# The end of the experts and the query norms of a two-block network: an earlier branch, column groups, weights split in the wait

## The reference

```python
def hier_moe(h, ...):                       # h: 768 rows in layer 0, 512 in layer 1
    # each row goes to 2 of 32 experts, with weights w
    y = sum_over_2( w * (silu(x @ w_gate[e]) * (x @ w_up[e])) @ w_down[e] )
x = x + g2 * y                              # in both layers
h = rmsnorm(x, norm_mix_g[1]) * (1 + sc1) + sh1          # start of layer 1
q, k, v, cq, ckv, kr = split(h @ w_in)
q = rope(rmsnorm(q.reshape(..., 4, 128), q_g))           # a norm per head
k = rope(rmsnorm(k.reshape(..., 2, 128), k_g))
# after layer 1: x = rmsnorm(x, final_norm_g), then rmsnorm(x, norm_ffn1) @ ffn1_w1, ffn1_w3
```

## Time and profile before

| | us |
|---|---|
| three runs | 3094.8, 3103.38, 3102.12 (median 3102.12) |
| the profiled execution | 3101.73 |
| its span in the trace | 3099.9 |
| PE busy | 2854.0 (92%) |
| VectorE, ScalarE, GpSimd busy | 1075.6, 754.5, 503.1 |
| mean granted TensorE clock | 0.949 of 2.4 GHz |

### The profile page before, as it was taken

How to read it: one execution, slowest core, us unless ns; L and a number is a source line. 1 busy time by engine, 2 the same in 40 slices (tenths; PEclk the granted TensorE clock), 3 DMA queues, 4 the chain that set the end, 5 groups by cost and what they waited for, 6 DMA issues and landing times.

```text
span 3099.9 us, 37034 instructions
## 1 busy us (share of the span) xinstructions
PE 2854.0 (92%) x15818; PEld 2010.1 (65%) x15818; DVE 1075.6 (35%) x2095; ACT 754.5 (24%) x1299; POOL 503.1 (16%) x503
## 2 busy tenths in 40 slices
PE   6989899989969899979999996999999889999997
PEld 4777756445457666765645445888875556788876
DVE  4973310000034644331010004333355654432334
ACT  4142211101123144221110113222211164331223
POOL 0000133322210034113332221000033051000000
PEclk9999999999969999979999997999999999999998
DMA  7613999999942132279999983323311201332321
GB/s 275 202 45 119 361 383 407 411 408 411 392 164 68 57 109 109 82 297 365 413 414 417 416 362 126 109 96 95 123 58 38 94 15 55 95 109 82 109 87 43
DMA packets 140522, 621.53 MB, mean 200 GB/s; under 512 B 14127, under 2 KB 95151, under 8 KB 106688
## 3 DMA queue, kind: packets, MB, share of 16 engines
...
## 4 chain that ended last, share of the span: by engine, by line
PE 74%; DMA 12%; DVE 7%; ACT 2%; issue 2%; POOL 1%; PEld 1%; DVEq 0%; SPq 0%; POOLq 0%; PEldq 0%; ACTq 0%
PE ps L92 71%; DMA ring<-in_exp_up,wix 8%; DMA hT<-in_exp_up,wix 3%; PE ps L95 3%; DVE scr L114 2%; ACT hT L98 1%; DVE scr L106 1%; DMA ring<-in_mod_w 1%; DVE scr L120 1%; PEld ps L92 1%; DVE ring_r L106 1%; DVE scr L117 0%; DVE hT_r L106 0%; DVE hT L114 0%; POOL yrows L139 0%
## 5 line engine op out<-in xcount | busy, mean ns | idle before, releaser
L92 PE MATMUL ps<-ring_r 128*128 128x512 f32 (+1 forms) x2688 | 779.4, 376 | 22.2 <-DVE hT_r L106 21.5
L92 PEld LDWEIGHTS ps<-ring_r 128*128 128x128 f32 x2688 | 496.9, 191 | 129.5 <-issue 35.7
L92 PE MATMUL ps<-ring,scr 128*64 128x512 f32 (+4 forms) x1984 | 447.8, 547 | 40.0 <-DMA ring<-in_mod_w 23.7
L92 PE MATMUL ps<-hT_r,ring_r 128*128 128x512 f32 (+1 forms) x1256 | 472.8, 376 | 0.0
L92 PEld LDWEIGHTS ps<-ring,scr 128*64 128x64 f32 (+2 forms) x1984 | 163.4, 145 | 236.8 <-issue 223.9
L106 DVE TENSOR_TENSOR scr<-scr,ps 64x512 f32<-64x512 f32 (+1 forms) x76 | 52.4, 690 | 761.7 <-ACT scr L98 434.2
L92 PE MATMUL ps<-scr_r,ring_r 128*128 128x512 f32 x1312 | 306.7, 390 | 0.3 <-issue 0.3
L92 PEld LDWEIGHTS ps<-scr_r,ring_r 128*128 128x128 f32 x1312 | 246.3, 188 | 52.3 <-issue 0.5
L92 PEld LDWEIGHTS ps<-hT_r,ring_r 128*128 128x128 f32 x1256 | 240.9, 192 | 43.3 <-issue 2.0
L106 DVE TENSOR_TENSOR ring_r<-ring,ring_r 128x2048 fp32r<-128x2048 f32 (+1 forms) x98 | 216.1, 2228 | 73.4 <-ACT ring_r L102 73.0
L102 ACT ACTIVATE ring_r<-ring 128x2048 fp32r<-128x2048 f32 (+1 forms) x102 | 186.4, 1835 | 181.2 <-DMA ring<-in_ffn_w 132.0
...
## 6 DMA issues: line engine op xcount, KB each, us to landing
...
```

Of the source, the lines that this page charges most:

```text
L92: return self.real.matmul(o, l, r, start=start, stop=stop) if self.real else Quiet()
```

## The change

- `overflow` takes `instead`, which is run in the branch without further blocks. GpSimd now drains and branches before the scatter of block 31; the scatter is the first thing in either branch. "further" is counted in the branch.
- SyncE issues the two early weights ahead of its wait for the results, and each tile's results in one transfer of 1 MB instead of two of 512 KB.
- ScalarE makes the early upper parts, then loads the table of the square root, before it weighs tile 0. VectorE makes the lower parts before its first sum of rows; GpSimd makes none. The gains of the next norm (`dve_gains`) and of the two norms (`dve_two_gains`) are computed there too.
- `sums`: the squares are the moving operand (128 columns), the stationary one has 32 columns (ones, or the gains in columns 0 and 1 of 32 and zeros), and the eight matmuls go to four groups of 32 rows of PSUM, two into each. ScalarE copies the 128x128 out (`groups`), and one matmul by `group_sum` adds the four groups into a column (`total_columns`), in PE's order one tile later.
- `act_adaln`: the upper part of the first input tile comes ahead of the shift of the second.
- Heads: the squares are the stationary operand, a column of ones goes through (`norm_sum`), so a sum is a column of 128 tokens. Root and reciprocal are taken on 128x4 or 128x2, and PE spreads the result with four or two matmuls (`norm_root`) at the position after; VectorE copies it to SBUF and scales. The rotation comes one position later.

```diff
-POOL_LOWER = [("at", 0), ("at", 1), ("ffn1_", 1, 0), ("ffn1_", 3, 0)]
...
-    def overflow(self, flag, body, *own):
+    def overflow(self, flag, body, *own, instead=None):
...
         with self.real.Else():
+            if instead:
+                self.met = dict(met)
+                instead()
...
-    def dve_adaln(e, name, l, which, gname, T, st, two=None, normed=False):
+    def dve_gains(e, name, l, which, gname):
...
+    def dve_adaln(e, name, l, which, gname, T, st, two=None, normed=False, gains=True):
+        if gains:
+            dve_gains(e, name, l, which, gname)
...
             act_norm(e, st)
-        for kt in range(9 if two else 8):
-            if kt < 8:
-                for r, (a, n) in enumerate(chunks(T)):
-                    e.wait_ge(*root_took(st, a, kt == 7, h_scaled, name, kt, a))
-                    i = e.activation(H(kt, a, n), H(kt, a, n), ACT.Identity, bias=mod(l, which, kt, r))
-                i.then_inc(*h_ready.up(name, kt))
-            if two and kt >= 1:
-                e.wait_ge(*h_ready.of(name, kt - 1))
-                e.copy(two(kt - 1)[0], H(kt - 1, 0, T)).then_inc(*h_hi.up(name, kt - 1))
+        def upper(kt):
+            e.wait_ge(*h_ready.of(name, kt))
+            e.copy(two(kt)[0], H(kt, 0, T)).then_inc(*h_hi.up(name, kt))
+        for kt in range(8):
+            for r, (a, n) in enumerate(chunks(T)):
+                e.wait_ge(*root_took(st, a, kt == 7, h_scaled, name, kt, a))
+                i = e.activation(H(kt, a, n), H(kt, a, n), ACT.Identity, bias=mod(l, which, kt, r))
+            i.then_inc(*h_ready.up(name, kt))
+            if two and kt != 1:
+                upper(max(kt - 1, 0))
+        if two:
+            upper(7)
...
         e.memset(Two.eps2, EPS ** 2)
+        e.tt(Two.gn, vec("fin_g", 0, 8), vec("n1", 0, 8), MUL)
+        e.tt(Two.g2, vec("fin_g", 0, 8), vec("fin_g", 0, 8), MUL)
+        step(e, e.memset(Two.gains, 0.0))
         e.memset(Two.gains[:, :, 0:1], 1.0)
-        step(e, e.tt(Two.g2, vec("fin_g", 0, 8), vec("fin_g", 0, 8), MUL))
-        e.ts(Two.gains[:, :, 1], Two.g2, EPS, ADD)
-        e.tt(Two.gn, vec("fin_g", 0, 8), vec("n1", 0, 8), MUL).then_inc(*dve_step.up("two_gains"))
+        e.ts(Two.gains[:, :, 1], Two.g2, EPS, ADD).then_inc(*dve_step.up("two_gains"))
...
                 wr.take(expert_slot(kind, b), "e", l, kind, b)
+        for key in early[l]:
+            early_load(e, key)
...
         for i in range(M.NT):
-            for q in range(2):
-                r = 768 * q + 128 * i
-                e.dma(moe_y(l, i, q), yrows[r:r + 128, :]).then_inc(*y_in[i].up(l, q, by=16))
+            e.dma(moe_y(l, i).rearrange("p (q c) -> p q c", q=2), yrows.rearrange("(q t p) c -> t p q c", q=2, p=128)[i]).then_inc(
+                *y_in[i].up(l, by=16))
+    def early_load(e, key):
+        if key[0] == "at":
+            raw_load(e, 3 + key[1] % 3, key, *At.jobs[key[1]])
+        else:
+            ffn_load(e, ffn1, ffn1.jobs.index(key[1:]))
...
                 store(b - 1)
-        store(31)
...
         first, end = 32, M.NB
+        pool_outputs(e, l, 31, *y_out[1].up(l, 31, by=16))
...
         e.wait_ge(*ov_y[l][(end - 1) % 2].of(l, end - 1))
+        e.drain().then_inc(*pool_step.up("further", l))
...
-    def moe_y(l, i, q):
...
+    def moe_y(l, i):
+        a = 2048 * i
         if l == 0:
-            return ring[:, 1024 * n:1024 * n + 1024]
-        return (hT[:, 1024 * n:1024 * n + 1024] if n < 6 else moes[l].xr[n - 6])
+            return ring[:, a:a + 2048]
+        return hT[:, a:a + 2048] if i < 3 else moes[l].xr01
...
                     c = 512 * h + 128 * j
-                    m = e.transpose(o[:, 128 * j:128 * j + 128], moe_y(l, i, 0)[:, c:c + 128], k("id"))
+                    m = e.transpose(o[:, 128 * j:128 * j + 128], moe_y(l, i)[:, c:c + 128], k("id"))
...
         def sums(i):
+            o = ps.take("y_square", l, i)
+            e.wait_ge(*ps.ready("y_square", l, i))
             e.wait_ge(*squared.of(st_m[l].name, i))
+            if l:
+                e.wait_ge(*dve_step.of("two_gains"))
+            for c in range(8):
+                j = c % 4
+                m = e.matmul(o[32 * j:32 * j + 32, 0:128], Two.gains[:, c, :] if l else k("ones")[:, 0:32],
+                             M.xt[i % 2][:, 128 * c:128 * c + 128], c < 4, c >= 4)
+            m.then_inc(*ps.fill("y_square", l, i))
+        def total_columns(i):
             w = l + 1
-            for c in range(8):
-                m = e.matmul(total[:, w * i:w * i + w], M.xt[i % 2][:, 128 * c:128 * c + 128],
-                             Two.gains[:, c, :] if l else k("ones")[:, 0:1], c == 0, c == 7)
-            m.then_inc(*(ps.fill(st_m[l].name, "sum") if i == M.NT - 1 else pe_step.up("y_square", l, i)))
+            e.wait_ge(*ps.emptied("y_square", l, i))
+            m = e.matmul(total[:, w * i:w * i + w], M.ab[i % 2][:, 0:128], group_sum[:, 0:w], True, True)
+            m.then_inc(*(ps.fill(st_m[l].name, "sum") if i == M.NT - 1 else pe_step.up("y_total", l, i)))
...
             turn(i)
-            if i:
+            if i >= 1:
                 sums(i - 1)
+            if i >= 2:
+                total_columns(i - 2)
         sums(M.NT - 1)
+        total_columns(M.NT - 2)
+        total_columns(M.NT - 1)
...
+        for key in early[l]:
+            part_upper(e, key)
+        e.activation(small[:, 8:9], one, ACT.Sqrt)
...
             if i >= 2:
-                e.wait_ge(*pe_step.of("y_square", l, i - 2))
+                e.wait_ge(*ps.filled("y_square", l, i - 2))
...
+        def groups(i):
+            if i >= 2:
+                e.wait_ge(*pe_step.of("y_total", l, i - 2))
+            e.wait_ge(*ps.filled("y_square", l, i))
+            e.copy(M.ab[i % 2][:, 0:128], ps.ap("y_square", l, i)[:, 0:128]).then_inc(*ps.empty("y_square", l, i))
         def weigh(i):
-            e.wait_ge(*y_in[i].of(l, 1))
-            e.activation(moe_y(l, i, 0), moe_y(l, i, 0), ACT.Copy, scale=M.w1[:, i, :]).then_inc(*act_step.up("y_first", l, i))
+            e.wait_ge(*y_in[i].of(l))
+            y = moe_y(l, i)[:, 0:1024]
+            e.activation(y, y, ACT.Copy, scale=M.w1[:, i, :]).then_inc(*act_step.up("y_first", l, i))
...
         weigh(1)
-        for i in range(M.NT - 1):
+        for i in range(M.NT):
...
             squares(i)
-        for key in early[l][0:1]:
-            part_upper(e, key)
-        squares(M.NT - 1)
-        for key in early[l][1:] if l == 0 else ():
-            part_upper(e, key)
+            if i:
+                groups(i - 1)
+        groups(M.NT - 1)
...
         dve_router(e, l)
-        if l == 1:
-            dve_two_gains(e)
...
             e.wait_ge(*dve_step.of("mod_b", M.mod.name))
+            dve_gains(e, "at_in", 1, 0, "nmix")
+        else:
+            dve_two_gains(e)
+        for key in early[l]:
+            part_lower(e, key)
...
         for i in range(M.NT):
-            e.wait_ge(*y_in[i].of(l, 1))
+            e.wait_ge(*y_in[i].of(l))
             e.wait_ge(*act_step.of("y_first", l, i))
-            y, z = moe_y(l, i, 0), moe_y(l, i, 1)
+            y, z = moe_y(l, i)[:, 0:1024], moe_y(l, i)[:, 1024:2048]
...
         e.drain()
-        e.overflow(nix[0:1, 16:17], lambda: pool_further(e, l), *own_signals)
-        e.drain().then_inc(*pool_step.up("further", l))
+        e.overflow(nix[0:1, 16:17], lambda: pool_further(e, l), *own_signals,
+                   instead=lambda: pool_outputs(e, l, 31, y_out[1].sem, 16))
...
+    At.root = [AM[:, 56:60], AM[:, 60:64]]
...
     def sp_attention(e):
-        for j in range(7):
+        for j in range(len(early[0]), 7):
...
-        def norm(n):
-            w = At.heads[n][3]
+        def norm_sum(n):
...
             e.wait_ge(*squared.of("head", n))
-            e.matmul(o[:, 0:w], k("ones"), At.sq[n % 2][:, 0:w], True, True).then_inc(*ps.fill("head_s", n))
-            ps.release("head", n)
+            for j in range(At.heads[n][3] // 128):
+                x = e.matmul(o[:, j:j + 1], At.sq[n % 2][:, 128 * j:128 * j + 128], k("ones")[:, 0:1], True, True)
+            x.then_inc(*ps.fill("head_s", n))
+        def norm_root(n):
+            o = ps.take("head_r", n)
+            e.wait_ge(*ps.ready("head_r", n))
+            e.wait_ge(*inverse.of("head", n))
+            for j in range(At.heads[n][3] // 128):
+                x = e.matmul(o[:, 128 * j:128 * j + 128], At.root[n % 2][:, j:j + 1].broadcast_to([128, 128]), k("id"), True, True)
+            x.then_inc(*ps.fill("head_r", n))
...
                 rope("kr", At.kr[:, 0:512], *ps.emptied("ck_p", 2, 0))
-            if n >= 2 and At.heads[n - 2][6]:
-                rope(n - 2, At.heads[n - 2][4], *ps.emptied("head", n - 2))
+            if n >= 2:
+                norm_root(n - 2)
+            if n >= 3 and At.heads[n - 3][6]:
+                rope(n - 3, At.heads[n - 3][4], *ps.emptied("head", n - 3))
             if n >= 1:
-                norm(n - 1)
```

(57 more changed lines are left out.)

20 lines of the change are left out of this document (8 added, 12 removed).

## The result

The changed kernel took 3077.71 us (median of 5 runs, 3074.09 to 3082.55), the kernel before 3102.12 (5 runs, 3094.8 to 3114.37): a ratio of 0.9919, 95% interval 0.9893 to 0.9945. Forecast were 3084.6 us; 17.1 us of gain were predicted and 24.4 came (24.0 between the two profiled executions, 3101.73 and 3077.71). Now and then an execution takes over 4000 us at a granted clock of 0.61 to 0.66; such runs are left out of the ratios.

The account below looks back on a forecast made before the run. TensorE makes 74% of the chain of waits; the change touches three stretches without its dense work. Gains of 7.9 (layer 0), 7.7 (layer 1) and 3.0 (heads), less hand-overs, give 17.1: 3084.6 us, own range 3079 to 3089, whole 3076 to 3096.

Parts of the forecast that it names:

- Branch and scatter: Experts' ends: release of result loads moves from 880.8 to 879.5-881.5; worth 0 to 1 us a layer, counted as nothing.
- the rival of late results: Experts' ends: last scatter lands 4 us later beside the weights, each layer starts 3 us later: 3090.6 us; chance 0.21.
- Early weights: Start of the experts' ends: two 1 MB weight loads ahead of the results delay VectorE's first sum of rows by 3.4 us.
- a landing that moves by over 5 us: Experts' ends: the forecast called itself wrong if the results' landing moved by over 5 us.
- Column groups: Experts' ends, each tile: sixteen records take 1.1 us instead of 3.41, small matmul 0.43; VectorE becomes the limit at 3.56 us.
- The 1.5 us set aside: Experts' ends: 0.15 us a tile for handing over between PE and VectorE, over ten tiles, taken off the gain.
- Drain at a change of mode: Experts' ends: estimated 0.1 us a tiling change, 2 us over ten tiles if PE limits; by the row nothing, which the sum used.
- Ends: Experts' ends: layer 0 gains 7.9 us at the root; layer 1 gains 5.4 at the root plus 2.3 to PE's start, 7.7.
- Table: Experts' ends: the 1.28 us load leaves the stretch from last sum to root and precedes ScalarE's weighing of tile 0.
- Heads: Attention's query and key heads: 3.0 us gained, ends 3.7 gained and 6 lost; spreading the roots costs PE 10.0 us.
- The rival of small products that pull the clock down in the heads: Attention heads: each head's small matmuls bring the clock down for 3 us; 6 lost instead of 3 gained, 3093.6 us; chance 0.11.
- The slower side: Experts' ends: column groups don't overlap, a tile takes PE 5.6 us instead of 5.0; 4.8 us lost, 3106.5 us; chance 0.06.

Follow-up runs that it names:

- results_first: Changed kernel with result loads ahead of the early weights, table load and ScalarE's and VectorE's splits moved too: 3073.74 us (0.9912); again 3076.55 us (0.9893).
- pool_half: Results loaded ahead of the early weights, and the second half of each sum of two result rows moved from VectorE to GpSimd: 3071.95 us (0.9872).
- after_again: The changed kernel run once more, unaltered, for a second trace in a later session on another chip: 3085.59 us (0.9928 to the kernel before).
- before_again: The kernel before the change run once more, unaltered, for a second trace: 3097.53 us in one run.
- sums_back: Changed kernel with the squares summed by sixteen one-column records a tile, as before: 3097.05 us (0.9987 to the kernel before).
- table_late: Changed kernel without ScalarE's early square root, so the table loads behind the last sum: 3084.93 us (0.9927), beside 3085.59 of the changed kernel.

## Why the prediction was right, and which sizes were off

- **Branch and scatter, counted at nothing.** The scatter starts 4.7 us behind the copy, where the forecast had it (877.8, or 4.8), and the release came 0.4 and 0.2 us earlier: in this kernel the edit is worth next to nothing, as forecast. It is not worth nothing by itself. With no weights ahead the release of layer 1 comes 1.7 us earlier than before, 5.8 us against 7.5 (both traces of results_first; 6.9 in pool_half), and that of layer 0 0.2 us. With the weights ahead it comes at 6.9 to 7.6 us in the traces that have the new branch: the scatter of layer 1 lands up to 1.5 us later beside them, a small piece of the rival of late results.
- **Early weights, forecast 3.4 us late at each start.** Measured 5.0 and 5.9 (in after_again 4.8 and 4.9), against the first trace of before; against before_again it is 3.2 and 4.9 (3.0 and 3.9), so in layer 0 the forecast is not clearly wrong. The step that was mis-sized is "4.9 us for the first": that was the first load of results, and the first early weight took 6.2 us (878.31 to 884.55) in layer 0 and 7.5 in layer 1. The next two took 3.6 and 3.2 us in layer 0, not 2.9. All that stands behind shifts: tile 0's data landed 17.6 us behind the copy in both layers, 4.9 and 5.1 later than in the first trace of before, and in layer 1 the table on ScalarE adds 0.8. That touches one of the forecast's own signs of being wrong, a landing that moves by over 5 us. That VectorE's lower parts end under it held. The cause is right in kind: with results ahead of the weights, and the splits behind them, results_first gets all of it back. Which of its moves does it is not tested one by one.
- **Column groups.** Forecast 1.1 us a tile at 1.2 GHz, measured 1.08; 3.41 without (sums_back). The small product 0.38 to 0.59 for 0.43. VectorE limits, at 3.39 us, not 3.56 plus 0.15: its two kinds overlap by 0.16 a tile, and with waits before PE's work nothing is lost in handing over. The 1.5 us set aside were not needed.
- **Drain at a change of mode.** The row's side held: the one-column product begins 1.01 us behind the start of sixteen records of 1.08 (903.26, 904.27), with no gap. The Trainium skill's rule (TensorEngine Tiling, Key Properties) would have cost nothing visible either way, since PE now waits for others in all tiles but one; no run here puts the drain on the path.
- **Ends.** Tiles 25.4 and 18.6 us against 37.1 and 27.6. Late start and tiles together give: 6.8 us at the root in layer 0 (forecast 7.9), 3.1 in layer 1 (5.4). From root to product in layer 1 2.3 us, exactly as worked out from GpSimd's split; in layer 0 0.6, where 0 to 0.5 were allowed for the upper part that is moved ahead.
- **Table.** Off the chain between last sum and root as said; but it stood in ScalarE's queue ahead of the first weighing, and table_late shows the two nearly even. The forecast had both terms, yet as if the start were paid already by the weights.
- **Heads, forecast 3.0, bounds -3.7 to 6: measured 7.0, and 5.4 in after_again.** The term that was mis-sized is the price of the roots: the row of "six blocks take 2.14 us" is a mixture of the two clocks, and the heads run at 2.4 GHz. Its first records start 0.213 us apart and the others 0.111; all at 1.2 GHz the same twelve take 2.93 us. A block of 128 columns takes 0.22 us of PE's time in the heads (four, in eight records, 0.89 us from start to start, 999.39 to 1000.28), so eight heads cost 6.2 us, not 10.0. With that, 55.2 + 6.2 + the wait of 1.93 is 63.3 and the gain 5.6, as six of the nine traces with these heads show (5.4 to 5.7); the 7.0 us of the first trace has the luck of a clock that did not fall. The forecast's sign that no wait over 0.3 us is left was wrong by this one wait: the product of piece 6 waits for a scaling on VectorE, which frees the bank. The clock rule that was weighed there (TensorE: Matmul & The Clock Gate, "Why this matters for your kernels", in the Trainium skill) says that idle gaps take the clock down, and agrees with the heads: the granted clock over them is 1.00 or 0.98 where before it was 0.96 (pool_half has 0.96 too), and all that is left of low clock stands behind the 1.93 us wait. It does not cover the ends, where the earlier trace rows has 1.2 GHz with no idle time. The rival of small products that pull the clock down in the heads is refuted: in none of nine traces do the products behind them slow down, save behind that wait.
- **The rest.** 4.3 of the 24.0 us (-0.7, -0.1, 3.5, 1.6) lie where nothing was changed. before_again shows 3.5 of them to be chance. In the stretch of the 1.6 before has a low clock at the start of the feed-forward block (granted 0.66 over 5 us) that the first trace of after does not have (1.00) and six traces of other changed kernels have again (0.89 to 0.92 over the first 24 us). But after_again has 1.00 there as well, and takes 1181.2 us to the end, more than before's 1178.9: this too is within chance.
- **The slower side.** By its own terms layer 0 of that rival is 5.6 us late, not 5.3 (3.4 + 3.7 + 0.3 - 1.8), and its time 3106.8 us; nothing hangs on it.

In sum: the mechanisms held, and of the rivals only late results came, in one layer and small. A term was too small by 4 (heads, 1.4 of it luck), two too large by 0.6 and 2.3 (ends), 1.5 were set aside for nothing, and 4.3 lie outside the change, which is luck: 4.0 - 0.6 - 2.3 + 1.5 + 4.3 = 6.9, the difference of 24.0 and 17.1. The forecast came as near as it did partly because its misses have both signs.
